# Scoring attention units two ahead, residue order beside the values, and a changed router chain in a two-layer encoder kernel

## The reference

```python
affinity = jax.nn.softmax(jnp.einsum('td,de->te', tokens, w_router), axis=-1)
gate, idx = lax.top_k(affinity.T, cap)          # 64 sample and 32 prompt tokens per expert
xe = tokens[idx]
hid = silu(einsum('ecd,edf->ecf', xe, w_gate)) * einsum('ecd,edf->ecf', xe, w_up)
ye = einsum('ecf,efd->ecd', hid, w_down) * gate[..., None]
out = zeros_like(tokens).at[idx.reshape(-1)].add(ye.reshape(-1, Dm))
```

## Time and profile before

| | |
|---|---|
| time, median of 3 runs | 1890.14 us (1889.2 to 1891.15) |
| profiled execution | 1889.91 us |
| its span, first to last instruction | 1888.1 us |
| mean granted TensorE clock | 0.949 of full speed |
| busy: PE, DVE, ACT, POOL | 92%, 70%, 59%, 13% of the span |
| chain that ended last | PE 87%, ACT 5%, DVE 4%, DMA 2% |

### The profile page before, as it was taken

How to read it: one execution, slowest core, us unless ns; L and a number is a source line. 1 busy time by engine, 2 the same in 40 slices (tenths; PEclk the granted TensorE clock), 3 DMA queues, 4 the chain that set the end, 5 groups by cost and what they waited for, 6 DMA issues and landing times.

```text
span 1888.1 us, 23209 instructions
## 1 busy us (share of the span) xinstructions
PE 1730.4 (92%) x9704; PEld 1351.7 (72%) x9704; DVE 1330.7 (70%) x1010; ACT 1117.7 (59%) x1165; POOL 239.2 (13%) x118
## 2 busy tenths in 40 slices
PE   6889889949999999999969988894999999999997
PEld 6878878936776776777749876793677767767765
DVE  4633445568888888888844455547788888888885
ACT  4343343237777777777744445522777777777774
POOL 0100000010011010010011000001031121221211
PEclk9989987969999999999979989996999999999999
DMA  4410213379999999999963102227899999999994
GB/s 155 110 32 29 65 46 122 120 280 359 389 388 372 392 389 376 394 380 386 389 166 91 40 15 48 78 99 265 329 378 386 388 373 388 391 377 390 388 385 148
DMA packets 155836, 485.91 MB, mean 257 GB/s; under 512 B 12199, under 2 KB 46119, under 8 KB 155687
## 3 DMA queue, kind: packets, MB, share of 16 engines
q1 hardware_dynamic: 148308, 459.26, 65.2%
q0 software_dynamic: 7424, 25.17, 5.6%
HBM read 454.26 MB, written 30.13 MB: 257 GB/s over the span
## 4 chain that ended last, share of the span: by engine, by line
PE 87%; ACT 5%; DVE 4%; DMA 2%; issue 1%; POOL 0%; SPq 0%; POOLq 0%; DVEq 0%; ACTq 0%
PE ps L1631 19%; PE ps L1633 19%; PE ps L1632 19%; PE ps L1378 5%; PE ps L1380 4%; PE ps L1379 4%; PE ps L1454 4%; PE ps L1543 2%; PE ps L1545 2%; PE ps L1544 2%; PE ps L1616 1%; ACT probs L847 1%; PE ps L1427 1%; PE ps L1443 1%; PE ps L1609 1%
## 5 line engine op out<-in xcount | busy, mean ns | idle before, releaser
L1195 DVE TENSOR_TENSOR w_lo<-ring,w_hi 128x2048 fp32r<-128x2048 f32 x384 | 876.7, 2290 | 158.8 <-ACT w_hi L920 158.6
L920 ACT ACTIVATE w_hi<-ring 128x2048 fp32r<-128x2048 f32 x384 | 735.8, 1918 | 280.4 <-PE ps L1633 280.4
L1631 PE MATMUL ps<-w_hi,xe_hi 128*96 128x512 f32 x1024 | 408.5, 399 | 3.8 <-DVE xe_lo L1293 3.8
L1633 PE MATMUL ps<-w_hi,xe_lo 128*96 128x512 f32 x1024 | 404.0, 394 | 0.0
L1632 PE MATMUL ps<-w_lo,xe_hi 128*96 128x512 f32 x1024 | 403.0, 394 | 0.0
L1631 PEld LDWEIGHTS ps<-w_hi,xe_hi 128*96 128x96 f32 x1024 | 166.1, 162 | 74.6 <-DVE xe_lo L1293 10.0
L1633 PEld LDWEIGHTS ps<-w_hi,xe_lo 128*96 128x96 f32 x1024 | 166.0, 162 | 72.3
L1632 PEld LDWEIGHTS ps<-w_lo,xe_hi 128*96 128x96 f32 x1024 | 166.5, 163 | 65.2
L1378 PE MATMUL ps<-c_hi,hT_hi 128*128 128x256 f32 x648 | 193.8, 299 | 10.2 <-DVE hT_lo L1007 3.5
L1631 PE MATMUL ps<-w_hi,hid_hi 128*96 128x512 f32 x512 | 201.7, 394 | 0.0
L1633 PE MATMUL ps<-w_hi,hid_lo 128*96 128x512 f32 x512 | 201.2, 393 | 0.0
(11 more groups left out here) (175 smaller groups left out, 2031.3 us busy)
## 6 DMA issues: line engine op xcount, KB each, us to landing
ring<-in_moe_w_gate SPq DMA_DIRECT2D x128, 1024.0 KB, 7.4
ring<-in_moe_w_up SPq DMA_DIRECT2D x128, 1024.0 KB, 8.5
ring<-in_moe_w_down SPq DMA_DIRECT2D x128, 1024.0 KB, 8.1
wbuf<-in_a_w_in SPq DMA_DIRECT2D x9, 1024.0 KB, 8.8
ffn_rows<-hrow SPq DMA_DIRECT2D x12, 512.0 KB, 2.7
wbuf<-in_b_w_in SPq DMA_DIRECT2D x5, 1024.0 KB, 7.0
unit_rows<-row SPq DMA_DIRECT2D x36, 132.0 KB, 1.7
bias<-bias_rows SPq DMA_DIRECT2D x4, 768.0 KB, 10.6
```

Source lines behind the costliest of these rows:

```text
L920: nc.scalar.activation(w_hi[:, n % SPLIT], ring[:, n % RAW], ACT.Copy).then_inc(hi_split, 1)
L1195: nc.vector.tensor_tensor(w_lo[:, n % SPLIT], ring[:, n % RAW], w_hi[:, n % SPLIT].bitcast(F32), ALU.subtract).then_inc(lo_split, 1)
L1631: nc.tensor.matmul(out, hi[:, k, :], w_hi[:, n % SPLIT, i, cols], start=(k == 0), stop=False)
L1633: ins = nc.tensor.matmul(out, lo[:, k, :], w_hi[:, n % SPLIT, i, cols], start=False, stop=(k == KM - 1))
```

## The change

In one kernel:

- **Scores.** In layer 0's groups 1 and 2 and in layer 1, scores(n + 2) are issued inside outputs(n), between the transposes of the first lots and the first product with the values. Layer 1 needs a third buffer of probabilities (half of `v`), and `row` gets a fourth. ScalarE takes unit n + 1's or n + 2's exponentials after unit n's lots.
- **Tiles.** Some projections also go between transposes and values. Layer 0: unit 0 has none, unit 1 six. Layer 1: the first unit of a group has all six.
- **Residue order.** Group 0's value tiles are projected sample first; VectorE folds the low parts from there on, and ScalarE folds four of its eight while the two prompt tiles are projected, four after unit 1's lots. Products on folded rows wait for one copy at a time.
- **Router.** The row goes to the router with the gain alone (`gain_row`), and 1/rms is put into the softmax's exponential; ScalarE scales the row later (`scale_rows`). TensorE's transposes and router products move one column part ahead. Three sample rounds go before the last `add_out`, two after it, three over both, and one over the prompt's 256 columns. The picks take four copies instead of ten. Row numbers are written before the weights.
- **Idle products.** 79 products (`idle_products`: 5, 4, 6, 28, 36) whose result nobody reads are put between the steps of the routing chain. The first product of expert 0 uses the high rows first.

```diff
+        def tile_at(chunk, j):
+            return ORDER[j] if chunk == FIRST_CHUNK[0] + 2 else j
...
-        TILES_BESIDE = [(3, 3, 3, 3, 3, 3), (2, 2, 2, 0, 0, 0)]
+        TILES_BESIDE = [[(0, 6, 3, 3, 3, 3), (3, 3, 3, 3, 3, 3)], [(6, 0, 0, 0, 0, 0)] * 2]
...
+        def scores_beside(layer, n):
+            g, i = n // NT, n % NT
+            if layer:
+                return [], [n + 2] if n + 2 < NU else [], []
+            behind = [n + 1] if i == NT - 1 and g < NG - 1 else []
+            if g == 0:
+                return [n + 1] if i < NT - 1 else [], [], behind
+            return [n + 1] if i == 0 else [], [n + 2] if i < NT - 2 else [], behind
+        def tiles_placed(layer, n):
+            tiles = tiles_beside(layer, n)
+            if layer == 0 and n == 1:
+                return [], [], tiles
+            if layer == 0 and (n < NT or n % NT == 0):
+                return tiles[:1], [], tiles[1:]
+            if layer and n == 0:
+                return tiles[:2], tiles[2:], []
+            return [], tiles[:1], tiles[1:]
...
+        def probs_of(layer, n):
+            if layer:
+                return v[:, 1].rearrange("p t c -> p (t c)") if n % 3 == 0 else probs[:, n % 3 - 1, :]
+            if n < NT:
+                return probs[:, n % 2, :]
+            return probs[:, 0, (n % 3) * GH * P:(n % 3 + 1) * GH * P]
+        def pitch_of(layer, n):
+            return P if layer == 0 and n >= NT else BAND
...
+                exps(0)
+                for n in range(NU):
+                    ahead, between, _ = scores_beside(layer, n)
+                    tiles_ahead, tiles_between, tiles = tiles_placed(layer, n)
...
+                    for c, t in tiles_ahead:
                         take_tile(c, t)
...
+                    for lot in batches[:2]:
+                        take_lot(lot)
+                    for c, t in tiles_between:
+                        take_tile(c, t)
+                    for lot in batches[2:]:
+                        take_lot(lot)
+                    if layer == 0 and n == 0:
+                        high_chunk(first + 3)
+                    if layer == 0 and n == 1:
+                        fold_high((3, 2, 1, 0))
+                    if layer and n == 0:
+                        exps(1)
+                    for m in ahead + between:
+                        exps(m)
+                    for c in ended_before(layer, n):
+                        high_chunk(c + 2)
+                    if n == 2 * NT + 1:
+                        high_chunk(FIRST_OUT[layer] + 2)
                     for c, t in tiles[:-1]:
                         take_tile(c, t)
                     for kind, b in turns[:2]:
...
                     for kind, b in turns[2:]:
                         take_heads(kind, b)
+                    for m in scores_beside(layer, n)[2]:
+                        exps(m)
...
+                def scale_rows(i):
+                    t = ORDER[i]
+                    act.wait_ge(rstd_ready, rstd_count(2 * layer + 1, i))
+                    nc.scalar.activation(hrow[:, t, :], hrow[:, t, :], ACT.Copy, scale=rstd[:, t:t + 1]).then_inc(row_scaled, 1)
                 def exp_route(part):
                     act.wait_ge(rlog_ready, 2 * layer + part + 1)
-                    nc.scalar.activation(lexp[:, STREAM[part], :], lgt[:, STREAM[part], :], ACT.Exp).then_inc(rexp_ready, 1)
+                    for t in range(STREAM[part].start, STREAM[part].stop):
+                        ins = nc.scalar.activation(lexp[:, t, :], lgt[:, t, :], ACT.Exp, scale=rstd[:, t:t + 1])
+                    ins.then_inc(rexp_ready, 1)
...
-                    dve.wait_ge(proj_done, 3 * NT)
+                    dve.wait_ge(proj_done, 2 * NT + NT - PT_)
...
+                if layer == 0:
+                    fold_low()
+                    dve.wait_ge(tab_out, 16)
+                logits(0)
+                if layer:
+                    logits(1)
+                for n in range(NU):
+                    ahead, between, _ = scores_beside(layer, n)
+                    if n:
+                        take_unit(n - 1)
+                        for m in scores_beside(layer, n - 1)[2]:
+                            logits(m)
+                    for m in ahead + between:
+                        logits(m)
                     if layer == 0 and n == 0:
                         low_chunk(first + 3)
-                        fold_low()
-                    if n:
-                        take_unit(n - 1)
...
+                def gain_row(i):
+                    t = ORDER[i]
+                    dve.wait_ge(attn_added, NT * layer + i + 1)
+                    nc.vector.tensor_tensor(hrow[:, t, :], x[:, t, :], gain[:], ALU.mult).then_inc(h_ready, 1)
...
+                def top_round(rows, r, last):
+                    cols, w = slice(8 * r, 8 * r + 8), DEC_SEQ if rows.start == 0 else SEQ
+                    best = pk_g[rows, cols]
+                    step(nc.vector.max(best, am[rows, 0:w]), route_step)
+                    step(nc.vector.max_index(topi[rows, cols], best, am[rows, 0:w]), route_step)
+                    if not last:
+                        step(nc.vector.match_replace(am[rows, 0:w], best, am[rows, 0:w], -1.0), route_step)
+                SAMPLE, BOTH, PROMPT = slice(0, NE), slice(0, 48), slice(32, 32 + NE)
...
-                    add_out(i)
                     if i == NT - PT_:
                         route_logits(0)
+                        affinities(0)
+                    if i == NT - 1:
+                        take_affinities(0)
+                        for r in range(3):
+                            top_round(SAMPLE, r, False)
+                    add_out(i)
+                    gain_row(i)
                     row_means(2 * layer + 1, i)
-                    if i == NT - PT_:
-                        affinities(0)
-                    ffn_row(i)
-                    if i == NT - PT_:
-                        take_affinities(0)
-                        top_round(0)
-                        top_round(1)
-                top_round(2)
-                top_round(3)
+                top_round(SAMPLE, 3, False)
+                top_round(SAMPLE, 4, False)
                 route_logits(1)
                 affinities(1)
                 take_affinities(1)
-                for r in range(4, CS // 8):
-                    top_round(r)
...
+                for r in range(5, CS // 8):
+                    top_round(BOTH, r, False)
+                top_round(PROMPT, (CS - CP) // 8, True)
+                nc.vector.tensor_copy(pk_i[SAMPLE, 0:CS], topi[SAMPLE, :])
+                nc.vector.tensor_copy(pk_i[PROMPT, CS:C], topi[PROMPT, CS - CP:CS])
+                nc.vector.tensor_copy(pk_i[PROMPT, 0:CP], topi[PROMPT, CS - CP:CS])
+                nc.vector.tensor_copy(pk_g[PROMPT, CS:C], pk_g[PROMPT, CS - CP:CS]).then_inc(picks_ready, 1)
                 dve.wait_ge(picks_turned, layer + 1)
...
+                nc.vector.tensor_scalar(take[0:CS, :], ps[0:CS, 5, 0:NE], float(SEQ), None, ALU.add)
+                nc.vector.tensor_copy(take[CS:C, :], ps[CS:C, 5, 32:48]).then_inc(slots_ready, 1)
...
+                nc.vector.tensor_copy(weight[0:CS, :], ps[0:CS, 5, 64:64 + NE])
+                nc.vector.tensor_copy(weight[CS:C, :], ps[CS:C, 5, 96:96 + NE]).then_inc(weight_ready, 1)
...
+                def idle_products(count):
+                    for i in range(count):
+                        nc.tensor.matmul(ps[:, 6, 0:P], ident[:], x[:, PT_, i % KM * P:(i % KM + 1) * P], start=True, stop=True)
...
+                        folding = layer == 0 and g == 1
+                        out, w, t = ps[:, proj_bank(n), 0:GW], chunk % 2, tile_at(chunk, t)
+                        for k in reversed(range(KM)) if folding else range(KM):
+                            if folding:
+                                pe.wait_ge(fold_hi_ready, KM - k)
+                                pe.wait_ge(fold_lo_ready, KM - k)
...
                     turn(0)
+                    if len(batches) > 1:
+                        turn(1)
+                    between()
                     for i in range(len(batches)):
-                        if i + 1 < len(batches):
+                        if 0 < i and i + 1 < len(batches):
...
+                def unit_of(n):
+                    ahead, between, behind = scores_beside(layer, n)
+                    tiles_ahead, tiles_between, tiles = tiles_placed(layer, n)
+                    turns = heads_beside(layer, n)
+                    for m in ahead:
+                        scores(m)
+                    for j, (c, t) in enumerate(tiles_ahead):
                         project(c, [t])
-                    outputs(n)
-                    tiles = tiles[first_tiles:]
-                    turns = heads_beside(layer, n)
+                        if layer and n == 0 and j == 0:
+                            scores(1)
+                    heads = lots
+                    def in_between():
```

(49 more changed lines are left out.)

136 lines of the change are left out of this document (51 added, 85 removed).

## The result

The changed kernel takes 1865.76 us (median of 4 runs, 1865.12 to 1869.2); beside it the kernel before took 1890.43 (4 runs, 1889.2 to 1891.15). The ratio is 0.9872, with a 95% interval of 0.9856 to 0.9889: 24.7 us faster, where 19.3 were forecast. The two profiled spans are 1888.1 and 1864.1 us, 24.0 apart.

The account below looks back on a forecast made before the run. Experts are TensorE-bound; time is won where TensorE idles or runs at lower clock, in attention and routing. Terms 2.0 + 2.9 + 3.4 - 3.0 + 14.0 = 19.3 us off 1889.91 gave 1870.6 us, range 1858 to 1881.

Parts of the forecast that it names:

- Folding: Layer 0, units 0 and 1: splitting the eight fold copies shortens TensorE's waits, gaining 2.0 us (1.4 to 3.7).
- Group 1: Layer 0, group 1: the 0.69 us lot wait is covered in six units, less 1.2 in unit 6; gains 2.9 us.
- Scores or a tile: Layer 0, group 1: either one between transposes and values covers the 0.69 us lot wait, 4.1 us in six units.
- Group 2: Layer 0, group 2: four units lose lot waits (1.9 us), up to 5.2 if the clock rises; gains 3.4 us.
- Layer 1: Layer 1's attention: take_unit stands behind VectorE's wait for GpSimd, TensorE idles about 4.5 us twice; loses 3.0 us.
- The first rival: Layer 1's attention: take_unit is not late and TensorE's idle time shrinks, +5 us, total 1862.6 us; chance 0.2.
- Routing: Routing stage, both layers: earlier gather, full-clock transposes and first products, no wait for low rows; gains 7.0 us a layer, 14.0.
- its 8.69 us stay: Routing stage: the gather still takes 8.69 us from its start, competing with the same weight loads as before.
- The rival by which the landing does not move: Routing: the gather lands when weight loads let it, so nothing of the 4.1 us is left; 1884 us, chance 0.05.
- the clock terms, 0.7 + 1.7 - 0.5: Routing, per layer: full-clock gathered-row transposes gain 0.7 us, first expert products 1.7, one possible clock fall costs 0.5.
- The fall counted at -0.5: Routing: the 2.4 us hole left after the 28 idle products may cost one clock fall, 0.5 us a layer.
- The rival of products in the way: TensorE's queue, last projection to gather: idle products at low clock delay experts; about 19 us slower, 1909 us, chance 0.05.

Follow-up runs that it names:

- the pair at 140.4 busy: Changed kernel with layer 0's group 2 scores one unit ahead (layer 1's attention 163.22 us), against changed kernel with layer 1's old order (161.52 us).

## Why the prediction was right, and where it was wrong

The total, 1870.6 against 1865.8, lies within the range (whose lower end is written as 1858, while the upper ends of the terms that it is said to come from give 1856.7). Without the 3.3 us of luck in the stretch to scores(0) the profiles are 20.7 apart, against 19.3 forecast. The terms are less good than their sum, in which misses of 1.9 to 3.3 us in both directions cancel by luck.

1. **Folding**, 2.0 forecast: scores(3) starts at 127.37 instead of 129.93, 2.6. The holes came where they were laid (before unit 1's transposes 2.04 for 1.6, before its lots 1.30 for 1.7, in the tile 0.95 for 0.5; the 2.7 before the second tile did not come), and the clock was at 1.2 GHz for 10 us, as allowed for. Not foreseen: another 1.3 us in the rest of group 0. No run has this part alone; it is read from the two traces.
2. **Group 1**, 2.9 forecast, 4.9 measured. All six 0.69 us went. The price in unit 6 was 1.35 at its tile for the 1.2 forecast, but one of the two tile waits there had been paid before. "Scores or a tile" was how the step named the cover: it is the tile. Scores two ahead give nothing more in group 1, where a tile lies there already, and what they win in group 2 is lost again (next item).
3. **Group 2**, 3.4 forecast, 0.1 measured: the step that failed. It counted what units 12 to 15 win, about 1.9, and that the clock might rise. They won 1.2, the clock stayed at 0.50, and 1.1 went on the way of unit 15's row through memory, which the step had taken as a constant.
4. **Layer 1**, -3.0 forecast, -5.2 measured in this pair of profiles, 4.5 of it idle time and 0.6 busy time; -1.7 in the pair at 140.4 busy. The mechanism was right: take_unit stands in VectorE's queue behind the wait for GpSimd, with a hole of 4.40 us at unit 9, as forecast at 4.5. In group 0 it came as 2.78 at unit 2 and 1.33 at unit 3, and four of the six tiles of each group wait 0.56 to 0.64, where five waits of 0.78 were forecast. The first rival (layer 1 gains) is out. The Trainium skill (TensorE: Matmul & The Clock Gate, Part 1) calls VectorE's queue strictly first in, first out, and the trace agrees: L1143 starts at 1141.65, right behind L1070. What the term lacked is the size of the clock: with one unit ahead the stage takes between 157.8 and 169.5 us with the old tiles, and 186.7 with six tiles in the first unit.
5. **Routing**, 14.0 forecast, 17.0 measured (8.6 and 8.4). The split was wrong. The chain alone gives 8.8 in each layer (no idle product against before), for 4.1 + 1.0 forecast. The gather is issued 3.7 us earlier after turn_mix(0) without the products and 5.35 with them (4.1 forecast). The rest is its landing: "its 8.69 us stay" was wrong for the change, where it took 6.3 and 4.6. The kernel before issues it 0.27 us after VectorE's first split has begun, and the issue alone takes 3.04 us; the changed kernel issues it 0.27 ahead of the split, in 1.15. The traces hold 24 gathers of the new chain, all issued in 1.0 to 1.15 us, and they landed 4.2 to 9.2 us after their start, so the short issue alone does not make an early landing. What goes with it is the load on the DMA engines in the 4 us after the issue: at a mean busy share of 1.03 to 1.08 (layer 0 with idle products, eleven gathers) it took 6.3 to 9.2, at 0.57 to 0.96 (the other thirteen) 4.2 to 5.7. In the old chain that share is 0.18 to 0.20 and the landing takes 8.4 to 8.7, so the load is not all of it; the cause was not tried. The rival by which the landing does not move is out all the same: in layer 0 it came 4.1 to 7.8 us earlier after turn_mix(0) than in the kernel before. And the clock terms, 0.7 + 1.7 - 0.5, are real (transposes 0.82 for 1.51, experts 1.7 to 1.9 shorter), but the 36 products outlast the gather (by 2.7 and 4.4 us in the changed kernel) and take as much back, 1.9 and 2.4 by the run without products. The fall counted at -0.5 came in both layers: behind the hole of 2.67 the clock was at 0.50 from 381.3 to 384, and the 36 products took 9.93 us for 8.6 forecast. The rival of products in the way was right in kind and wrong in size: 0.23 us each at full clock, and no fall beyond that one.
6. **Not in the sum**: 3.3 us at the start of layer 1, by the clock, in this pair of profiles.

The Trainium skill (DMA: Bandwidth & Descriptors, Anatomy of one DMA) gives an estimate of 2.9 us for the gather. The fastest seen here took 4.2, with the DMA engines busy at 0.57 in the 4 us after its issue; the others took 4.3 to 9.2, so no run here agrees with the estimate. What the prediction drew from it, that the products would outlast the gather, came true.

## What to carry to other kernels

A copy that TensorE waits for can be covered by independent work put between its producer and its consumer, here a projection tile; ask first whether the work that is there already, moved by one place, does it, before scheduling more of it ahead. Before a term is counted, follow the chain that ends the stage: here a row's way through memory took back what denser units won. Work that only keeps the clock up has to end before the thing waited for, in its fastest case as well, or it takes back what it gives; and when a change is measured, cut the runs at fixed marks, since a clock that falls at chance places moves the total by more than most edits.

## What the hardware showed unexpectedly

- The same products of layer 1's attention kept TensorE busy for 136 us at a mean granted clock of 0.92 and 163 at 0.77. With scores two units ahead the stage ended in 163.0 to 163.5 us in nine kernels, at 136.8 busy and 26.2 idle as at 140.4 and 22.8; with one ahead it took 157.8 to 186.7 in five.
- Parts of a change did not add: 9.4 and 4.7 us alone, 24.7 together, although the stage gains add up within 0.5 us in all but one stage.
- A single gather of 96 rows took from 4.2 to 9.2 us to land, and its issue on GpSimd 1.0 to 3.0. With the same 1.15 us issue in layer 0 it landed in 4.6 (DMA engines busy at 0.74 in the 4 us after) and in 9.2 (at 1.08).
